# Filler blocks in quarters between the steps of the gated heads of a two-block transformer, on one Trainium2 core

## The chip, the cores and the metric

The program runs on one core of a Trainium2 chip. The metric is the device time of the whole program in microseconds, lower is better. The kernel before takes 3076.76 us (median of 3 runs, 3075.69 to 3077.55). The core's engines run side by side and are joined by semaphores only: TensorE (PE in the profile), VectorE (DVE), ScalarE (ACT), GpSimd (POOL) and the queue that loads weights (SP).

## The reference

A first block (two layers of feed-forward, hybrid mixer, feed-forward) is followed by a second one. The change touches only the token mixer of the second block. There the latent tokens (512) and the context tokens (256) go through one projection `w_in`; a latent attention (MLA) and a gated linear attention (GLA) follow, and both are merged under gates:

```
k_nope_c, v_c = mla_keys_values(kv_cc, kv_norm_g, w_ukv)      # context, norm of 2 x 128 features
k_nope, v = mla_keys_values(kv_c, kv_norm_g, w_ukv)           # latent, the same norm
q_nope, q_rope = mla_queries(q_c, q_norm_g, w_uq)             # norm of 3 x 128 features
s_f = gla_final_state(kg_c, vg_c, gf_c, s0)                   # context: states alone
s_b = gla_final_state(flip(kg_c), flip(vg_c), flip(gb_c), s0)
o_gla, _, _ = gla_bidirectional(qg, kg, vg, gf, gb, s_f, s_b) # latent: states and outputs
out_lat = merge_branches(o_mla @ w_br_mla, gla_branch(o_gla, gr, gla_norm_g, w_br_gla), gate_logits, w_out)
```

One direction of a gated head works in chunks of 64 tokens:

```
b_cum = cumsum(g)                                   # g = log_sigmoid(low-rank product + bias) / 16
u = (kc * exp(b_last - b_cum)).T @ vc               # one update per chunk
s = exp(b_last) * s + u                             # chain over the chunks
a = (qc * exp(b_cum)) @ (kc * exp(-b_cum)).T * mask # scores inside a chunk
o = a @ vc + (qc * exp(b_cum)) @ s_in
y = rms_norm(o) * silu(r)                           # per head, over its 128 values
```

There are four heads and two directions, for the context (states only) and for the latent tokens.

## The kernel before, in words

**Blocks.** All large products are cut into blocks of 1024 rows x 256 columns of weights (1 MB each, `raw`, four slots). ACT writes the high part of a block (`split_hi`, L919), POOL the low part (`split_lo`, L403), and TensorE takes three products for each of 8 x 2 tiles: 48 products of 128x512 (`products`, L452 to L475, lines L468 to L470). Blocks alternate between two places for weights and two pairs of PSUM banks. A half of the weights of block k+2 may be written once block k has passed its middle (`front_done`), the other once it is done (`block_done`). ACT's `evac` of block k writes the first half of block k+2, waits for the end of block k, copies its two results and writes the second half. All these wait in ACT's own order; POOL has one order of splits and of `rms` steps (`rstd`, L408), written out by hand.

**Fillers.** Blocks 8 to 13 and 21 to 29 are independent of the heads and are set between their steps. `FILLERS[u]` lists those of head u (0 to 3 context, 4 to 7 latent tokens), `KVX_FILLER` and `QX_FILLER` are those inside which the column sums of the two norms lie. Fillers 9 to 13 and 27 to 29 are gate logits, copied and spilled by a DMA from ACT; 21 to 26 are the keys, queries, values and `gr` of the next heads.

**Context head u** on TensorE (`gla_context`): a filler; a wait for the state chain of the head before; `gla_updates`, that is three groups of transposes (`turn`, L692), a wait for ACT's copies of them (`turn_ready`) and the update products (L717); `gla_pre` of the next head (decay product, L698); a second filler, if there is one. After head 1 come block 11 with the column sums of the keys' norm, its rows, and a wait for the normed keys (`kvn_ready`); after head 2 block 13 with the queries' norm and a wait for `qn_ready`. The norm itself is DVE's `norm_split`.

**Token head h** on TensorE (`gla_tokens`, u = 4 + h): a filler, in whose middle the rows of the norm of the head before are made (`rms_rows`, L506); turns, wait, updates; the second filler; a wait for the first direction's chain, the score products (L741); a wait for both chains and for the masked scores (`am_ready`); the outputs (L748, L752); the decay product of the next head; the column sums of this head's norm (`rms_cols`, L487), which wait for ACT's square of the outputs. ACT per head: `gla_decays` (three exponentials), filler, `gla_turned` (copies of the turns), filler, square and copy of the outputs, `gla_logs` of the next head (abs, exp, ln). DVE per head: `gla_chain` (two chains of 8 steps, L1680 and L1687), masks (L1720, L1723), `rms_var`, `gla_cumulate` of the next head (L1641 to L1653), `gla_out` (L1708, L1711), `gla_weigh` (L1662 to L1668). After head 3 follow block 29 with the rows of its norm, and the branch products (L899).

## Time and profile before

| | |
|---|---|
| median of 3 runs | 3076.76 us |
| profiled execution | 3074.51 us, span 3072.7 us |
| TensorE busy | 2875.3 us (94%), mean granted clock 0.957 |
| DVE, ACT, POOL busy | 1463.0 (48%), 997.7 (32%), 1132.7 us (37%) |
| context heads | about 2026 to 2148 us |
| token heads | about 2394 to 2585 us |

A busy share is a mean over the whole program. Idle time of TensorE inside the two stretches is read from its waits and from its timeline. The granted clock is the share of full speed (2.4 GHz) at which TensorE ran in a stretch.

### The profile page before, as it was taken

The numbers are of one execution on the slowest core, as the hardware profiler recorded it, in microseconds if no ns is written. First come the engines' busy times: TensorE is split into PE (matmuls) and PEld (weight loads), VectorE is DVE, ScalarE is ACT, GpSimd is POOL, SyncE is SP. The second block draws the span as 40 slices with busy tenths as digits, with TensorE's granted clock in tenths as the row PEclk, the third lists the DMA queues.
The fourth block names the chain that finished last, engine by engine and source line by source line (L and its number), as shares of the span: only waits on it lengthen the run. The fifth ranks groups of instructions, "written<-read, shape, count | busy, mean of one in ns | idle before, by whom it ended". The sixth has DMA issues, their size and how long they took to land.

```text
span 3072.7 us, 36418 instructions
## 1 busy us (share of the span) xinstructions
PE 2875.3 (94%) x12748; PEld 2290.3 (75%) x12748; DVE 1463.0 (48%) x2627; ACT 997.7 (32%) x1409; POOL 1132.7 (37%) x488
## 2 busy tenths in 40 slices
PE   7999999899999999999899999897788899999998
PEld 4888877688887888877678888775444777788886
DVE  3534366452525525265644335625454445563735
ACT  2222235332223322235432222342333443242422
POOL 2444443244444444443244444442111213334443
PEclk9999999999999999999999999897899888999998
DMA  6535442243535435352135344432000113322221
GB/s 247 205 112 184 143 151 69 83 137 137 183 141 197 139 135 190 138 179 81 43 116 188 133 163 165 162 126 77 28 28 28 55 41 130 123 83 94 97 96 41
DMA packets 69266, 374.32 MB, mean 122 GB/s; under 512 B 7776, under 2 KB 8544, under 8 KB 38656
## 3 DMA queue, kind: packets, MB, share of 16 engines
q1 hardware_dynamic: 65424, 359.61, 33.3%
q10 hardware_dynamic: 3696, 12.85, 1.1%
q8 instruction: 81, 1.33, 0.2%
q14 instruction: 65, 0.53, 0.1%
HBM read 364.04 MB, written 8.39 MB: 121 GB/s over the span
## 4 chain that ended last, share of the span: by engine, by line
PE 39%; issue 32%; POOL 19%; DVE 4%; ACT 2%; DVEq 1%; ACTq 1%; SPq 1%; DMA 1%; POOLq 0%
POOL w_lo L403 19%; PE psum L468 10%; PE psum L469 10%; PE psum L470 10%; PE psum L850 1%; PE psum L828 1%; PE psum L717 1%; PE psum L752 1%; PE psum L840 1%; DVE psum L1842 1%; PE psum L698 1%; ACT w_hi L919 0%; PE psum L901 0%; PE psum L899 0%; PE psum L900 0%
## 5 line engine op out<-in xcount | busy, mean ns | idle before, releaser
L403 POOL TENSOR_TENSOR w_lo<-raw,w_hi 128x1024 fp32r<-128x1024 f32 x464 | 1114.1, 2407 | 1769.5 <-ACT w_hi L919 1769.5
L468 PE MATMUL psum<-h_hi,w_hi 128*128 128x512 f32 x2256 | 898.4, 398 | 25.5 <-DVE h_lo L1363 16.6
L469 PE MATMUL psum<-h_lo,w_hi 128*128 128x512 f32 x2256 | 891.5, 395 | 0.0
L470 PE MATMUL psum<-h_hi,w_lo 128*128 128x512 f32 x2256 | 889.8, 394 | 0.0
L919 ACT CAST w_hi<-raw 128x1024 fp32r<-128x1024 f32 x464 | 482.2, 1048 | 941.7 <-PE psum L470 815.3
L468 PEld LDWEIGHTS psum<-h_hi,w_hi 128*128 128x128 f32 x2256 | 432.3, 192 | 122.9 <-DVE h_lo L1363 15.8
L470 PEld LDWEIGHTS psum<-h_hi,w_lo 128*128 128x128 f32 x2256 | 431.6, 191 | 91.4
L469 PEld LDWEIGHTS psum<-h_lo,w_hi 128*128 128x128 f32 x2256 | 432.6, 192 | 89.9 <-issue 0.5
L468 PE MATMUL psum<-hid_hi,w_hi 128*128 128x512 f32 x880 | 350.4, 398 | 4.7 <-DVE hid_lo L1848 4.7
L470 PE MATMUL psum<-hid_hi,w_lo 128*128 128x512 f32 x880 | 350.1, 398 | 0.0
L469 PE MATMUL psum<-hid_lo,w_hi 128*128 128x512 f32 x880 | 350.1, 398 | 0.0
L1390 DVE SCALAR_TENSOR_TENSOR x<-psum,gate,x 128x512 f32<-128x512 f32 x128 | 90.2, 747 | 390.7 <-PE psum L470 355.4
L1304 DVE SCALAR_TENSOR_TENSOR psum<-mod_raw,psum 128x512 f32<-128x512 f32 x336 | 255.5, 760 | 37.8 <-issue 18.5
L1408 DVE TENSOR_TENSOR psum<-act_ring,psum 128x512 f32<-128x512 f32 x88 | 61.3, 696 | 403.6 <-ACT act_ring L941 403.6
L468 PEld LDWEIGHTS psum<-hid_hi,w_hi 128*128 128x128 f32 x880 | 166.7, 189 | 46.1 <-DVE hid_lo L1848 6.0
L469 PEld LDWEIGHTS psum<-hid_lo,w_hi 128*128 128x128 f32 x880 | 166.7, 189 | 40.1
L470 PEld LDWEIGHTS psum<-hid_hi,w_lo 128*128 128x128 f32 x880 | 166.5, 189 | 40.2
L941 ACT ACTIVATE act_ring<-psum 128x512 f32<-128x512 f32 x88 | 52.7, 599 | 372.2 <-PE psum L470 372.1
L1842 DVE SCALAR_TENSOR_TENSOR psum<-gpad,cpar,psum 128x441 f32<-128x441 f32 (+2 forms) x176 | 123.2, 700 | 13.6 <-issue 0.6
L408 POOL TENSOR_TENSOR rstd<-var,mhalf 128x4 f32<-128x4 f32 x18 | 18.5, 1029 | 158.0 <-DVE var L1341 158.0
L1415 DVE TENSOR_TENSOR hid_lo<-psum,hid_hi 128x512 fp32r<-128x512 f32 x88 | 60.5, 688 | 31.9 <-ACT hid_hi L947 31.9
L1321 DVE CUSTOM_DVE_ANT_0 mod_acc<-psum,ident 128x128 f32<-128x128 f32 x208 | 54.1, 316 | 34.4 <-DMA alibi<-in_alibi_dram 14.8
(337 smaller groups left out, 2843.4 us busy)
## 6 DMA issues: line engine op xcount, KB each, us to landing
raw<-in_weights_dram SPq DMA_DIRECT2D x232, 1024.0 KB, 5.6
mod_raw<-in_mod_w_dram SPq DMA_DIRECT2D x192, 512.0 KB, 4.2
first_mods_a<-in_mod_w_dram SPq DMA_DIRECT2D x8, 512.0 KB, 11.8
first_mods_b<-in_mod_w_dram SPq DMA_DIRECT2D x8, 512.0 KB, 15.3
first_mods_a<-gate_spill ACTq DMA_DIRECT2D x4, 1024.0 KB, 10.8
gate_spill<-gate_out_c ACTq DMA_DIRECT2D x5, 512.0 KB, 3.0
x<-in_xT_dram SPq DMA_DIRECT2D x1, 2048.0 KB, 8.7
x_spill<-x ACTq DMA_DIRECT2D x1, 2048.0 KB, 11.5
```

Source lines behind the costliest of these rows:

```text
L403: pool.tensor_tensor(w_lo[:, k % 2, cs], raw[:, k % 4, cs], w_hi[:, k % 2, cs].bitcast(F32), ALU.subtract).then_inc(lo_ready, 1)
L468: pe.matmul(out, wh, rhs_hi[:, c, :], start=(c == ks[0]), stop=False)
L469: pe.matmul(out, wh, rhs_lo[:, c, :], start=False, stop=False)
L470: mm = pe.matmul(out, wl, rhs_hi[:, c, :], start=False, stop=(c == ks[-1]))
L919: act.copy(w_hi[:, k % 2, cs], raw[:, k % 4, cs]).then_inc(hi_ready, 1)
L941: act.activation(act_ring[:, j % 2, :], psum[:, 2 * (k % 2), :], ACT.Silu).then_inc(silu_ready, 1)
L1304: o = dve.scalar_tensor_tensor(macc, w, cond_ps[:, k:k + 1], macc, ALU.mult, ALU.add)
L1321: dve.tensor_tensor_reduce(mod_acc[:, t * P:(t + 1) * P], psum[:, bank, t * P:(t + 1) * P], ident[:, :], 1.0, 0.0, ALU.mult, ALU.add, mod_ ...
L1390: o = dve.scalar_tensor_tensor(x[:, m, :], psum[:, 2 * (k % 2) + t, :], gate[:, m:m + 1], x[:, m, :], ALU.mult, ALU.add)
L1408: dve.tensor_tensor(ps, act_ring[:, j % 2, :], ps, ALU.mult).then_inc(prod_ready, 1)
L1415: dve.tensor_tensor(hid_lo[:, j, :], ps, hid_hi[:, j, :].bitcast(F32), ALU.subtract).then_inc(hid_ready, 1)
L1842: dve.scalar_tensor_tensor(dst[:, rs, cs], src[:, rr, cc], tap(3 * (dy + 1) + dx + 1), dst[:, rs, cs], ALU.mult, ALU.add)
```

## The change

The fillers are dealt out anew. A new helper `quarters` issues a block in parts of 12 products, so that small steps can stand between parts. In the token heads the first filler is run by `beside_norm`, which sets the column sums of the head before behind its first quarter and the rows behind its third; `gla_updates` is cut in two, `gla_turns` and `gla_updates`, with the first quarter of the second filler between; the second quarter stands ahead of the scores, the last two behind them. The decay product of the next head now stands ahead of the outputs; on ACT `gla_logs` stands ahead of the square. On DVE the variance step lies inside `gla_cumulate`. In the context heads every head has one filler, blocks 10 and 12 carry the norms' column sums, and the waits for `kvn_ready` and `qn_ready` stand behind the next filler. POOL's order of `rms` steps and splits follows the blocks.

```diff
-FILLERS = ((8, 9), (10,), (12,), (), (21, 22), (23, 24), (25, 26), (27, 28, 29))
-KVX_FILLER, QX_FILLER = 11, 13
+FILLERS = ((8,), (9,), (11,), (13,), (21, 22), (23, 24), (25, 26), (27, 28, 29))
+KVX_FILLER, QX_FILLER = 10, 12
 ...
-            for r, k, n in (..., (R_KVC, 8, 5), (R_KVX, 13, 2), (R_QX, 15, 8)):
+            for r, k, n in (..., (R_KVC, 8, 4), (R_KVX, 12, 2), (R_QX, 14, 9)):
 ...
+            def quarters(g, k, qs, rhs):
+                for q in qs:
+                    wait_block(g, k, q // 2)
+                    if q == 0:
+                        pe.wait_ge(out_free[k % 2], 2 * g + k // 2 + 1)
+                    for c in (2 * q, 2 * q + 1):
+                        for t in range(2):
+                            wh, wl = (w[:, k % 2, c * 256 + t * P:c * 256 + (t + 1) * P] for w in (w_hi, w_lo))
+                            out = psum[:, 2 * (k % 2) + t, :]
+                            pe.matmul(out, wh, rhs[0][:, c, :], start=(c == 0), stop=False)
+                            pe.matmul(out, wh, rhs[1][:, c, :], start=False, stop=False)
+                            mm = pe.matmul(out, wl, rhs[0][:, c, :], start=False, stop=(c == KC - 1))
+                    if q == 1:
+                        mm.then_inc(front_done, 1)
+                    if q == 3:
+                        mm.then_inc(block_done, 1)
 ...
             def gla_context(u):
-                if len(FILLERS[u]) > 0:
-                    products(G2, FILLERS[u][0], hx)
+                products(G2, FILLERS[u][0], hx)
                 if u:
                     pe.wait_ge(chain_ready, 2 * u)
-                gla_updates(u, gv_c[:, u, :], TC)
+                if u == 2:
+                    pe.wait_ge(kvn_ready, 2)
+                if u == 3:
+                    pe.wait_ge(qn_ready, 1)
+                gla_turns(u, gv_c[:, u, :], TC)
+                gla_updates(u, TC)
                 if u < 3:
                     gla_pre(u + 1, glow_c, TC)
-                if len(FILLERS[u]) > 1:
-                    products(G2, FILLERS[u][1], hx)
+
+            def beside_norm(k, h):
+                quarters(G2, k, (0,), hx)
+                if h >= 0:
+                    rms_cols(R_GLA + h, T, ssq, O_BANK)
+                quarters(G2, k, (1, 2), hx)
+                if h >= 0:
+                    rms_rows(R_GLA + h, T, O_BANK - 1)
+                quarters(G2, k, (3,), hx)
 
             def gla_tokens(h):
                 u, pairs = 4 + h, T // P
-                products(G2, FILLERS[u][0], hx, between=(lambda: rms_rows(R_GLA + h - 1, T, O_BANK - 1)) if h else None)
-                gla_updates(u, gv[:, h % 2, :], T)
-                products(G2, FILLERS[u][1], hx)
+                beside_norm(FILLERS[u][0], h - 1)
+                gla_turns(u, gv[:, h % 2, :], T)
+                quarters(G2, FILLERS[u][1], (0,), hx)
+                gla_updates(u, T)
+                quarters(G2, FILLERS[u][1], (1,), hx)
                 pe.wait_ge(chain_ready, 2 * u + 1)
 ...
                 mm.then_inc(a_ps, 1)
+                quarters(G2, FILLERS[u][1], (2, 3), hx)
                 pe.wait_ge(chain_ready, 2 * u + 2)
                 pe.wait_ge(am_ready, h + 1)
+                if h < GLA_HEADS - 1:
+                    gla_pre(u + 1, krope, T)
 ...
                 mm.then_inc(og_ps, 1)
-                if h < GLA_HEADS - 1:
-                    gla_pre(u + 1, krope, T)
-                rms_cols(R_GLA + h, T, ssq, O_BANK)
 ...
-            products(G2, FILLERS[7][2], hx, between=lambda: rms_rows(R_GLA + GLA_HEADS - 1, T, O_BANK - 1))
+            beside_norm(FILLERS[7][2], GLA_HEADS - 1)
 ...
                 filler(FILLERS[u][1])
+                if h < GLA_HEADS - 1:
+                    gla_logs(u + 1, T)
                 act.wait_ge(og_ps, h + 1)
                 act.activation(ssq[:, :], psum[:, T_BANK, :], ACT.Square)
 ...
-                if h < GLA_HEADS - 1:
-                    gla_logs(u + 1, T)
 ...
                 dve.tensor_tensor(prod[:, :, W], t_ring[:, :, W], act_ring[:, :, W], ALU.subtract)
                 dve.drain()
+                if meanwhile is not None:
+                    meanwhile()
 ...
-                    gla_cumulate(u + 1, T)
+                    gla_cumulate(u + 1, T, lambda: rms_var(R_GLA + h, T, P, O_BANK))
```

## Rows read from the trace of the kernel before

**Rows 1.** The page: busy us (share of the span) x instructions.
```profile
PE 2875.3 (94%) x12748; PEld 2290.3 (75%) x12748; DVE 1463.0 (48%) x2627; ACT 997.7 (32%) x1409; POOL 1132.7 (37%) x488
```
**Rows 2.** TensorE's waits, 2340 to 2620: us in total, times, longest.
```profile
PE psum L717 <- ACTq L1114: 10.7, 4, 3.2
PE psum L748 <- DVE am L1723: 10.4, 4, 3.6
...
PE psum L692 <- DVEq L1663: 2.9, 1, 2.9
```
**Rows 3.** TensorE's waits, 2000 to 2160.
```profile
PE psum L717 <- ACTq L1114: 8.8, 4, 2.6
PE psum L692 <- DVEq L1663: 7.6, 1, 7.6
PE psum L468 <- DVEq L1599: 5.8, 1, 5.8
```
**Rows 4.** Windows: us; busy of PE, PEld, DVE, ACT, POOL; clock; DMA share, GB/s.
```profile
503.00:519.00 16.00, 15.94 (x86) 11.95 (x88) 12.52 (x29) 7.41 (x25) 4.80 (x2) 1.00 0.19 67
2412.00:2459.00 47.00, 39.64 (x218) 33.15 (x217) 23.28 (x35) 20.48 (x24) 10.94 (x5) 0.89 0.13 45
2505.00:2555.00 50.00, 45.00 (x215) 37.08 (x214) 23.28 (x35) 20.49 (x24) 10.93 (x5) 0.80 0.15 53
```
**Rows 5.** TensorE's timeline, token heads: start us, duration, instruction, [idle before].
```profile
2387.39 0.39 PE L468 MATMUL psum<-h_hi,w_hi 128*128 128x512 f32 x1
...
2392.83 0.39 PE L468 MATMUL psum<-h_hi,w_hi 128*128 128x512 f32 x1
...
2393.52 0.60 PE L692 MATMUL psum<-ident,gv 128*128 128x128 f32 x4
...
2397.53 3.27 PE L717 MATMUL psum<-gvt,kdT 64*128 64x128 f32 x32 [2.54 <-ACTq L1114]
...
2412.14 1.95 PE L741 MATMUL psum<-qe,kn 128*128 128x128 f32 x16
2416.32 1.13 PE L748 MATMUL psum<-am,gvt 128*128 128x128 f32 x8 [2.24 <-DVE am L1723]
...
2422.81 1.05 PE L487 MATMUL psum<-ones,ssq 128*128 128x1 f32 x8
...
2555.48 1.95 PE L741 MATMUL psum<-qe,kn 128*128 128x128 f32 x16
...
2585.31 0.40 PE L899 MATMUL psum<-om_hi,w_hi 128*128 128x512 f32 x1
```
**Rows 6.** ACT's timeline between token heads 0 and 1.
```profile
2415.06 1.04 ACT L919 CAST w_hi<-raw 128x1024 fp32r<-128x1024 f32 x1 [0.23 <-issue]
...
2422.92 1.27 ACT L1092 ACTIVATE act_ring<-psum,par 128x512 f32<-128x512 f32 x2 [0.63 <-PE psum L698]
...
2429.03 1.28 ACT L1101 ACT_TABLE_LOAD   x1
```
**Rows 7.** Timelines of DVE and, last, POOL, token heads 0 and 1.
```profile
2399.46 1.62 DVE L1687 SCALAR_TENSOR_TENSOR states<-states,prod,psum 128x128 f32<-128x128 f32 x4
...
2429.04 1.41 DVE L1641 TENSOR_SCALAR t_ring<-psum,par 128x512 f32<-128x512 f32 x2 [4.98 <-ACT act_ring L1096]
...
2435.72 0.75 DVE L1708 SCALAR_TENSOR_TENSOR y_gla<-o_sb,par,psum 128x512 f32<-128x512 f32 x1 [0.19 <-issue]
...
2439.98 2.85 DVE L1667 SCALAR_TENSOR_TENSOR qe<-gq,prod 128x512 f32<-128x512 f32 x1
...
2439.84 5.20 POOL L403 TENSOR_TENSOR w_lo<-raw,w_hi 128x1024 fp32r<-128x1024 f32 x2 [14.69 <-ACT w_hi L919]
```
**Rows 8.** Timelines of DVE (first) and TensorE, context heads 1 and 2.
```profile
2053.60 0.76 DVE L1653 TENSOR_TENSOR t_ring<-act_ring 128x256 f32<-128x256 f32 x2
...
2097.72 0.80 PE L468 MATMUL psum<-h_hi,w_hi 128*128 128x512 f32 x1 [5.78 <-DVEq L1599]
...
2110.35 0.38 PE L692 MATMUL psum<-ident,gv_c 128*128 128x128 f32 x2
```

More of the change, by code:

```diff
@@ L427, in _ @@
                         splits(g, k0 + 1, blocks)
-            for r, k, n in ((R_FINAL1, 1, 0), (R_CTX, 1, 4), (R_X1, 5, 3), (R_KVC, 8, 5), (R_KVX, 13, 2), (R_QX, 15, 8)):
+            for r, k, n in ((R_FINAL1, 1, 0), (R_CTX, 1, 4), (R_X1, 5, 3), (R_KVC, 8, 4), (R_KVX, 12, 2), (R_QX, 14, 9)):
                 rms(r)
@@ L700, in gla_pre, with gla_turns @@
                 mm.then_inc(pre_ps, 1)
-            def gla_updates(u, v_src, width):
+            def gla_turns(u, v_src, width):
                 pairs = width // P
-                kt, vt = (kdT, gvt) if width == T else (kdT_c, vt_c)
                 pe.wait_ge(qk_ready, u + 1)
@@ L712, in gla_updates @@
                 turn(psum[:, T_BANK + 1, :], t_ring[:, 1, :], pairs).then_inc(turn_ps, 1)
+            def gla_updates(u, width):
+                pairs = width // P
+                kt, vt = (kdT, gvt) if width == T else (kdT_c, vt_c)
                 pe.wait_ge(turn_ready, u + 1)
@@ L782, in _ @@
                     rms_rows(R_KVX, T)
-                    pe.wait_ge(kvn_ready, 2)
                 if u == 2:
@@ L786, in _ @@
                     rms_rows(R_QX, T)
-                    pe.wait_ge(qn_ready, 1)
             pe.wait_ge(chain_ready, 8)
@@ L1117, in gla_context @@
                 gla_decays(u, TC)
-                if len(FILLERS[u]) > 0:
-                    filler(FILLERS[u][0])
+                filler(FILLERS[u][0])
                 gla_turned(u, TC)
@@ L1122, in gla_context @@
                     gla_logs(u + 1, TC)
-                if len(FILLERS[u]) > 1:
-                    filler(FILLERS[u][1])
             def gla_tokens(h):
@@ L1631, in final_and_ctx_norm, with gla_cumulate @@
                 whole_norm(48, range(3, DC))
-            def gla_cumulate(u, width):
+            def gla_cumulate(u, width, meanwhile=None):
                 h, chunks = u % 4, width // GLA_CHUNK
@@ L1731, in gla_tokens @@
                     dve.drain()
-                rms_var(R_GLA + h, T, P, O_BANK)
                 if last:
+                    rms_var(R_GLA + h, T, P, O_BANK)
                     for c in range(GLA_HEADS - 1):
```

## The prediction

> **What bounds the kernel now.** Read the busy shares first: TensorE is busy 94% of the span [rows 1]. So only what leaves TensorE idle, or running at the lower of its two clock levels, can be won; a faster DVE, ACT or POOL is worth nothing unless TensorE waits for it. Then the waits of TensorE, cut to the two stages that the diff touches. In the gated heads of the latent tokens TensorE stood 10.7 us for the copies of the turned operands (`turn_ready`), 10.4 us for the masked scores (`am_ready`) and 2.9 us for the weighted keys (`qk_ready`) [rows 2]. In the four context heads it stood 7.6 us in one piece ahead of head 3's turns, 5.8 us in one piece ahead of the filler product of head 2, and 8.8 us in four waits for turned copies [rows 3]. Then the granted clock: 0.89 over one head's 47 us and 0.80 over another's 50 us, against 1.00 in a stretch of the mixer where quarters of a block alternate with small matmuls [rows 4]. With two levels, 2.4 and 1.2 GHz, 0.89 means 22% of the time at the lower one, 0.80 means 40%. Last the timelines of each engine over one head, for the sums below [rows 5 to 7].
>
> **The pieces on TensorE at the full level** [rows 5]. 24 products take 2392.83 - 2387.39 = 5.44 us, so a quarter (12) takes 2.7; I book 2.8, since each quarter begins behind small matmuls, and 5.5 for two together. Turns 1.5 us; updates 3.2 (x32, 3.27 with the overlap at their end); scores 1.95; outputs and decay product (`gla_pre`) together 2422.81 - 2416.32 = 6.5, of which 1.9 the decay product; column sums (`rms_cols`) 0.9 and rows (`rms_rows`) 0.8, each 1.05 with its overlap.
>
> **First token head, from its turns to the end of its second filler.** Turns 1.5. A quarter now stands between turns and updates; before, TensorE stood from the end of the turns to 2397.53, 4.0 us after the turns began at 2393.52. Turns and quarter are 4.3 us, so that wait is gone. Updates 3.2. Next a quarter of 2.8, then the wait for the first direction's state chain, which DVE starts halfway through the updates. Eight steps of 0.4 (states row of [rows 7]: 1.62 us for four, plus a copy of 0.3) are 3.4 us; from halfway that is 1.8 us behind the updates, inside the quarter's 2.8. Scores 1.95, two quarters 5.5. DVE's second chain (3.4) and its mask operations (2.2, the gap from the scores' end at 2412.14 + 1.95 to the outputs at 2416.32) end about 2.5 us before the quarters do, so the `am_ready` stall is gone as well. Sum 1.5 + 2.8 + 3.2 + 2.8 + 2.0 + 5.5 = 17.8.
>
> **One period, from the end of a second filler to the end of the next** (t = 0 at the start). The decay product stands first, 1.9, then outputs to 6.5, a quarter to 9.3. Now the column sums need ACT's square, and ACT is in order: the evacuation of the filler, from TensorE's end at 2412.14 to the end of the cast at 2415.06 + 1.04, occupies it to t = 4.0; the decay logs moved ahead of the square take 2422.92 to 2429.03, 6.1 us, to t = 10.1; then the square, 0.6 [rows 6]. Column sums at 10.9: a **new wait of 1.6 us**. Sums to 11.8, two quarters to 17.3, rows to 18.1, a quarter to 20.9. DVE: logs ready at 10.1, cumulation 6.6 us (2429.04 to about 2435.6, with the variance now inside it, 0.2), the norm and the weighing of keys 3.0 us (2435.72 to TensorE's turns at 2438.73) after the rows at 18.2: turns can start at 21.2, a **new wait of 0.3** [rows 7]. Turns to 22.7, quarter to 25.5 (ACT's turned copies are ready near 25.0: its decays end at 19.8, then a cast, two copies, a cast and three copies follow), updates 28.7, quarter 31.5, scores 33.5, quarters 39.0. DVE's query and key products run into POOL's splits there and end near 27.5; its chains then end at 31.0 and 34.4, the masks at 36.5: no wait. Three periods are 117.0, where the trace has 143.3 from 2412.14 to its third successor.
>
> **Last head**: outputs 4.6, quarter 2.8, sums 0.9, two quarters 5.5, rows 0.8, quarter 2.8, and 0.4 for the last norm and split (3.3 us on DVE behind the rows, a quarter of 2.8 and the sum's latency over it): 17.8. **Stage**: 17.8 + 117.0 + 17.8 = 152.6 against 2585.31 - 2393.52 = 191.8 [rows 5]: 39.2 us less, if the clock stays at the full level. It won't wholly. A drop came once a stall had preceded small matmuls; two of the three kinds of stall go, but pre, outputs and the 1.6 us wait lie close together, and at the lower level outputs and pre take 6.5 us longer together at worst. Bounds: nothing (the mixer's 1.00), or all of what was lost before, some 19 us (0.11 and 0.20 of 47 and 50 us [rows 4], less where TensorE was idle anyway, over four heads). I take 6, nearer the mixer row, whose pattern this becomes: **33 us**.
>
> **Context heads.** The fillers move so that a whole one stands behind each norm: block 11 between the norm of the keys and head 2's turns, block 13 between the norm of the queries and head 3's. A filler is 10.9 us; the waits are 5.8 and 7.6 [rows 3]: both covered, -13.4. Head 3 had no filler ahead of its turns, and its wait for the turned copies was 8.8 - 3 x 2.6 = 1.0; with a filler to evacuate first it becomes the 2.6 of the others: +1.6. Behind the 5.8 us stall 48 products took 2110.35 - 2097.72 = 12.6 us instead of 10.9 [rows 8]: -1.7. Head 1 loses one of two fillers: its keys must be weighed within the 10.9 us of block 9. Before, its cumulation was done at 2053.60 + 0.76 = 2054.4 [rows 8], and exponential and weighing (0.63 + 0.76) would have been done by 56.0, but ACT took them only behind the second filler; now ACT takes them at once, 2 us before TensorE arrives at about 58.1: no wait. The POOL passes and weight loads move along with their blocks; each split has the same lead of a block as before. The two waits moved from behind the norms to ahead of the turns queue only the turns behind them. Sum **-13.5 us**; bounds -10 (block 9 just misses) and -17 (the slow turns and updates behind the 7.6 us stall recover too).
>
> **Forecast.** 33.2 + 13.5 = 46.7. The profiled execution took 3074.5 us (span 3072.7); the median of the runs is 3076.8, 2.3 above it. 3074.5 - 46.7 = 3027.8, as a run 3030.
>
> **A rule weighed.** Between abs, exp and ln ACT shows 6.1 us for 1.27 + 1.28 + 1.06 + 1.28 + 1.06 = 5.95: the two table loads cost 1.3 us each and nothing more [rows 6]. The Trainium skill (ScalarE: Activation LUTs, What ACT_TABLE_LOAD costs) adds a drain of about 1.38 us to every switch. By it the square, now behind both, would come 2.8 us later in each of three heads, 8.3 us, and the time would be 3038; the trace decides against it. Should the square itself need a load behind ln (behind silu it didn't), that is 1.3 us a head.
>
> **Rivals.** (1) *The weighing falls behind POOL's split.* With POOL at work (5.2 us for two) one DVE product of two SBUF operands takes 2.85 us instead of 0.69 [rows 7]. In my sum the weighing ends 0.1 us after the cast that releases POOL, its last operation having begun 0.5 us before it. If the rows come 0.6 us later, the weighing loses one or two such operations, 2.2 to 4.9 us, in three heads: 6.6 to 15 us, 3037 to 3045. For it: the margin is thin, a short spell at the lower clock uses it up. Against: ACT's cast then starts no earlier, and before the change the order held in each of three heads. The Trainium skill (SBUF — State Buffer, Who interferes with whom) has this as an exclusive lock, taken by whoever issues first, for two-input operations too; by that rule, with which the 2.85 us agree, the loser waits whole operations, and the time is this rival's. (2) *The square is the new bound.* If the clock falls at every decay product, the outputs end later, but the square is bound by ACT; the pieces behind it run slow, some 6 us a head instead of 2: 18 more, the time 3042 to 3048. For it: 0.80 in the third head. Against: the stall that opened those spells is gone. (3) *Slower.* Cut into quarters, the products no longer hold the clock: each of the 432 products of nine blocks would cost another 0.227 us, 98 us in all. The gain before any clock loss, 39.2 + 13.5 = 52.7, is used up from 232 products at the lower level; with all of them the time is 3076.8 - 53 + 98 = 3122. For it: 0.80. Against: the mixer's quarters at 1.00. (4) *The filler hides nothing*, since DVE, not order, is the bound and the stalls move to the column sums: 3065 to 3080. Against: DVE is busy 23.3 us of 47 [rows 4].
>
> **How the numbers follow.** Forecast 0.62, with its own range 3022 to 3038; rival 1 0.14, rival 2 0.15, rival 3 0.04, rival 4 0.05. Range 3020 to 3046: it leaves out the two last, part of rival 2, and a gain beyond full clock and the context's upper bound. Within 0.2% is 3070.6 to 3082.9, about what a measurement can tell from no change: part of rival 4, 0.03. Slower 0.04 (rival 3), faster 0.93.
>
> **What would show it.** In the trace after: the waits for `am_ready` and of the updates in the token heads gone; a wait of column sums for ACT's square, 1 to 2.5 us, in heads 1 to 3; block ends 39 to 42 us apart; no wait of over 4 us in the context heads; four waits of 2.6 us for turned copies there. It is wrong if the turns wait more than 2 us, if the clock in the heads stays under 0.9, or if head 1's context turns wait for their weighed keys.

## The result

The changed kernel takes 3019.47 us (median of 4 runs, 3019.32 to 3021.84) against 3076.69 us before (median of 4 runs with the one made beside it). The ratio is 0.9815, 95% interval 0.9804 to 0.9827: 57.2 us less. I had forecast 3030 with a range of 3020 to 3046. The direction was right; the time lies 0.5 us below the range and 10.5 us below the forecast.

Where the time went is read from four marks in both traces: the first context decay product, the first value product behind the context heads, the first turn of token head 0, and the first branch product.

| stretch | before | after | difference | forecast |
|---|---|---|---|---|
| context heads | 2025.90 to 2147.82 = 121.9 | 2025.75 to 2130.68 = 104.9 | 17.0 | 13.5 |
| attention (unchanged code) | 2147.82 to 2393.52 = 245.7 | 2130.68 to 2376.15 = 245.5 | 0.2 | 0 |
| token heads | 2393.52 to 2585.31 = 191.8 | 2376.15 to 2532.20 = 156.1 | 35.7 | 33.2 |
| behind them (unchanged code) | 2585.31 to 3072.7 = 487.4 | 2532.20 to 3017.7 = 485.5 | 1.9 | 0 |

With 0.2 us ahead of the context heads that is the 55.0 us between the spans. The other 2.2 us between the medians are no change of the kernel: the profiled execution of before (3074.5) lay 2.2 us under its own median, that of after (3019.5) lay on it.

TensorE's waits in the token heads of the changed kernel, over 2330 to 2535 us (line, releaser: us in total, times, longest), answer to [rows 2]:

```profile
PE psum L710 <- DVEq L1696: 2.9, 3, 2.3
PE psum L505 <- ACTq L1167: 2.8, 3, 1.0
PE psum L487 <- ACTq L1091: 2.7, 1, 2.7
PE psum L777 <- DVEq L1729: 2.1, 2, 1.2
PE psum L933 <- DVEq L1771: 0.4, 1, 0.4
PE psum L716 <- DVE am L1756: 0.2, 1, 0.2
```

The update products (L739 now) no longer wait for turned copies. The masked scores (am) cost 0.2 us instead of 10.4. New are the waits of the column sums (L505) for ACT's square, 0.8 to 1.0 us in each of three heads, which the prediction had, and two waits of the scores (L777) for the state chain, which it had not. The turns (L710) wait 0.3 us in two heads as booked, and 2.3 us in head 3, where 0.3 was booked. In the context heads, over 2000 to 2160 us, answering to [rows 3]:

```profile
PE psum L739 <- ACTq L1148: 10.3, 4, 2.6
...
PE psum L831 <- DVEq L1729: 3.5, 1, 3.5
```

The waits for the two norms are gone, and head 3's wait for copies is as long as the others' now. The granted clock, as in [rows 4] (us; busy of PE, PEld, DVE, ACT, POOL; clock; DMA share, GB/s): before over the whole stretch of the token heads, then after over the same.

```profile
2394.00:2585.00 191.00, 166.34 (x857) 140.38 (x855) 90.30 (x143) 70.16 (x85) 43.66 (x20) 0.85 0.14 50
```
```profile
2376.00:2532.00 156.00, 147.78 (x862) 121.16 (x860) 88.52 (x143) 70.42 (x86) 46.47 (x20) 0.97 0.17 61
```

0.85 of 191 us means 57 us at the lower level, 0.97 of 156 means 9. The three periods, from decay product to decay product (in the last to the outputs of head 3, which has none), took 40.8, 38.3 and 42.7 us. The second on TensorE (start, duration, instruction, idle before):

```profile
2433.34 1.95 PE L716 MATMUL psum<-mod_acc,gates_all 32*128 32x512 f32 x4 [0.21 <-DVE am L1756]
...
2443.47 1.05 PE L505 MATMUL psum<-ones,ssq 128*128 128x1 f32 x8 [0.77 <-ACTq L1167]
...
2454.06 0.66 PE L710 MATMUL psum<-ident,gv 128*128 128x128 f32 x4 [0.30 <-DVEq L1696]
...
2458.30 2.06 PE L739 MATMUL psum<-gvt,kdT 64*128 64x128 f32 x32
2460.28 0.50 PE L487 MATMUL psum<-h_hi,w_hi 128*128 128x512 f32 x1
...
2464.18 2.05 PE L777 MATMUL psum<-qe,kn 128*128 128x128 f32 x16 [0.89 <-DVEq L1729]
...
2471.64 1.98 PE L716 MATMUL psum<-mod_acc,gates_all 32*128 32x512 f32 x4
```

This period took 38.3 us, where I had booked 39.0. The column sums come 10.1 us behind the decay product (10.9 booked), the turns 20.7 (21.2). The other two are longer: the three together took 121.8 us, where 117.0 were booked and, for the whole stage, 6 for the clock. In the first and in the third the two quarters behind the column sums ran in part at the lower level. Windows from the column sums to the rows, in the first period and then in the second:

```profile
2402.93:2411.02 8.09, 8.09 (x33) 6.66 (x34) 5.81 (x8) 3.86 (x5) 1.85 (x1) 0.79 0.02 7
2443.47:2449.96 6.49, 6.49 (x33) 5.51 (x34) 5.82 (x8) 2.25 (x3) 1.85 (x1) 1.00 0.02 6
```

In the third period they took 8.09 us again, and behind the turns' wait of 2.3 us the way from turns to updates took 5.85 us instead of 4.24. That is three times 1.6 us at the lower level, 4.8 in all. The updates take 2.0 us, not the 3.2 that I had read from [rows 5].

### The profile page after: what moved, and what is told of

It is laid out like the page before. It is cut to its first block, busy times and chain, and to the rows that moved or that the text cites. A ratio compares the mean times of both kernels' runs of the same rounds, so it can differ in the third digit from the quotient of the medians.

```text
span 3017.7 us, 36418 instructions
## 1 busy us (share of the span) xinstructions
PE 2846.8 (94%) x12748; PEld 2261.4 (75%) x12748; DVE 1463.1 (48%) x2627; ACT 997.9 (33%) x1409; POOL 1136.1 (38%) x488
## 4 chain that ended last, share of the span: by engine, by line
PE 39%; issue 33%; POOL 20%; DVE 4%; ACT 2%; DVEq 1%; ACTq 1%; DMA 1%; SPq 1%; POOLq 0%
POOL w_lo L403 20%; PE psum L468 10%; PE psum L470 10%; PE psum L469 10%; PE psum L884 1%; PE psum L862 1%; PE psum L487 1%; PE psum L488 1%; PE psum L489 1%; PE psum L874 1%; DVE psum L1875 1%; PE psum L933 1%; PE psum L935 0%; PE psum L934 0%; SPq L364 0%
## 5 line engine op out<-in xcount | busy, mean ns | idle before, releaser
L468 PE MATMUL psum<-h_hi,w_hi 128*128 128x512 f32 x2112 | 833.3, 395 | 17.2 <-DVE h_lo L1394 16.6
L469 PE MATMUL psum<-h_lo,w_hi 128*128 128x512 f32 x2112 | 829.1, 393 | 0.0
L470 PE MATMUL psum<-h_hi,w_lo 128*128 128x512 f32 x2112 | 828.3, 392 | 0.0
L468 PEld LDWEIGHTS psum<-h_hi,w_hi 128*128 128x128 f32 x2112 | 401.5, 190 | 106.9 <-DVE h_lo L1394 15.9
L469 PEld LDWEIGHTS psum<-h_lo,w_hi 128*128 128x128 f32 x2112 | 401.5, 190 | 83.8 <-issue 0.5
L470 PEld LDWEIGHTS psum<-h_hi,w_lo 128*128 128x128 f32 x2112 | 400.9, 190 | 84.6
## 6 DMA issues: line engine op xcount, KB each, us to landing
first_mods_a<-gate_spill ACTq DMA_DIRECT2D x4, 1024.0 KB, 10.9
```

The source lines that it names most:

```text
L468: pe.matmul(out, wh, rhs_hi[:, c, :], start=(c == ks[0]), stop=False)
L469: pe.matmul(out, wh, rhs_lo[:, c, :], start=False, stop=False)
L470: mm = pe.matmul(out, wl, rhs_hi[:, c, :], start=False, stop=(c == ks[-1]))
```

## The experiments

Gains below are against the changed kernel's median (3019.5), or, where said, against before's runs on the same chip. Where an edit touches one stage, its stretch in the trace tells more than the total: in these traces the code ahead of the context heads, the attention and the last stage move by 3 to 5 us, though nothing in them was changed.

### Each part alone

`ctx_only` has the change's context heads, waits and POOL order, `tok_only` its token heads; the other stage is as before.

```diff
 # ctx_only: against the kernel before, only this part of the change
-FILLERS = ((8, 9), (10,), (12,), (), ...)
-KVX_FILLER, QX_FILLER = 11, 13
+FILLERS = ((8,), (9,), (11,), (13,), ...)
+KVX_FILLER, QX_FILLER = 10, 12
+                if u == 2:
+                    pe.wait_ge(kvn_ready, 2)
+                if u == 3:
+                    pe.wait_ge(qn_ready, 1)
 # tok_only: all of the change but this part
```

> The context part alone: its fillers, waits and POOL order as in the changed kernel, the token heads as before. Theory A (the two parts are independent, and each is worth what its stretch of the two traces shows): the context stretch was 121.9 us and is 104.9, so 17.0 us less than before, near 3059.7. Theory B (my prediction's term, 13.5 us, with nothing regained behind the 7.6 us stall): near 3063. Rival C (the stretches share something, so that one part alone is worth less): above 3065. In the trace TensorE should have no wait for the normed keys or queries, and four of 2.6 us for turned copies.

> The token part alone: the context heads as before. Theory A: the token stretch was 191.8 us and is 155.5, so 36.3 less, near 3040.4. Theory B (my prediction's term): 33 less, near 3043.5. Rival C: under 30 us less, above 3046. With ctx_only the two gains should add up to the 55 to 57 us of the whole change; if they add up to less than 52, the parts help each other.

Measured: ctx_only 3059.48 us, ratio 0.9945 (0.9928 to 0.9961), 16.1 us under its own runs of before (3075.56). tok_only 3037.91 us, ratio 0.9877 (0.9861 to 0.9894), 37.7 us under them. Theory A holds for both; the sum, 53.8 us, is within the intervals of the whole's 57.2 (each reaches some 5 us to either side). The stretches show the independence more sharply: ctx_only has context heads of 105.2 us and token heads of 191.9 (104.9 after, 191.8 before), tok_only 121.8 and 156.1 (121.9 before, 156.1 after). Both terms of my sum were too small, neither wrong in kind.

### The price of the two norm stalls

```diff
             def gla_context(u):
+                if u == 2:
+                    pe.wait_ge(kvn_ready, 2)
+                if u == 3:
+                    pe.wait_ge(qn_ready, 1)
                 products(G2, FILLERS[u][0], hx)
                 if u:
                     pe.wait_ge(chain_ready, 2 * u)
-                if u == 2:
-                    pe.wait_ge(kvn_ready, 2)
-                if u == 3:
-                    pe.wait_ge(qn_ready, 1)
```

> The changed kernel with its two waits for the normed keys and queries put ahead of their fillers (blocks 11 and 13) again. It prices the two stalls alone, the order of the blocks unchanged. Theory A (a stall costs its own length and a spell at the lower clock behind it): waits of about 5.8 and 7.6 us come back, and the 48 products behind each take 12 to 13 us instead of 10.8; in all 16 to 17 us more than the changed kernel, near 3036. Theory B (the stall's own length is the whole cost): 13.4 us more, near 3032.9. If the waits come out much shorter than 5.8 and 7.6, the order of the blocks had changed their length.

Measured: 3038.81 us, ratio 0.9882 (0.9865 to 0.9898), 19 us more than the changed kernel (two runs near 3036.4 and two near 3041.2; the trace is of one near 3036.4). TensorE's waits over 2000 to 2160 us in this kernel:

```profile
PE psum L468 <- DVEq L1630: 12.4, 2, 6.6
```

and the filler behind the first of them, up to head 2's turns, on its timeline:

```profile
2086.83 0.80 PE L468 MATMUL psum<-h_hi,w_hi 128*128 128x512 f32 x1 [5.78 <-DVEq L1630]
...
2099.69 0.38 PE L710 MATMUL psum<-ident,gv_c 128*128 128x128 f32 x2
```

The stalls are 12.4 us long; the stretch (2025.86 to 2148.86 = 123.0 us) is 18.1 us longer than in the changed kernel. The other 5.7 us stand behind the stalls: 48 products take 12.86 us here and 11.0 without a stall ahead (2080.70 to 2091.71 in the changed kernel's timeline), the second time 12.78. From the rows ahead of a stall to the turns behind its filler the way is 7.9 us longer for the stall of 5.8, and 8.6 for that of 6.6: 1.3 to 1.4 times its length. The last 1.6 us lie between the two, in the decay product and the filler behind head 2's updates; that the stalls caused them is not shown. Theory A, and its price was if anything low.

### A stall ahead of the outputs

```diff
                 gla_updates(u, T)
-                quarters(G2, FILLERS[u][1], (1,), hx)
+                quarters(G2, FILLERS[u][1], (1, 2, 3), hx)
                 pe.wait_ge(chain_ready, 2 * u + 1)
 ...
                 mm.then_inc(a_ps, 1)
-                quarters(G2, FILLERS[u][1], (2, 3), hx)
```

> The changed kernel with all of the second filler's remaining quarters ahead of the scores, so that nothing stands between scores and outputs: the old place of the scores. Theory A (a stall ahead of small matmuls is what lowers the clock, so a stall costs more than its length): waits of 2.2 us for the masked scores come back in four heads, 8.8 us, the scores' waits for the first chain (2.1 us) go; on top the columns and products behind run at the lower clock in most heads, 4 to 8 us: near 3032. Theory B (the clock follows the share of idle time over the whole head, which changes little): the waits' length alone, 6.7 us, near 3026. Rival (the small matmuls themselves lower the clock, stall or not): the clock in the token heads stays at about 0.96 and the time is that of theory B.

Measured: 3040.07 us, ratio 0.9883 (0.9866 to 0.9899), 20.6 us more. Its waits over 2325 to 2545 us, and its clock over the token heads:

```profile
PE psum L716 <- DVE am L1755: 6.7, 3, 2.2
...
PE psum L786 <- DVE am L1755: 3.6, 1, 3.6
PE psum L710 <- DVEq L1695: 3.1, 3, 2.5
```
```profile
2383.00:2549.00 166.00, 152.56 (x792) 128.36 (x791) 86.32 (x137) 67.19 (x79) 43.48 (x19) 0.87 0.16 57
```

The waits came back at 10.3 us. The scores' and column sums' 4.9 us went, and the turns' and the branch products' stayed, so that all waits in the stage grew by 5.4 us (13.8 against 8.4). Yet the stage grew from 156.1 to 176.0 us, by 19.9. The rest is the clock, 0.87 in place of 0.97 over the stage. The outputs show it, first without and then with the drop, in heads 0 and 1 of this one kernel:

```profile
2397.64 3.68 PE L790 MATMUL psum<-qe,states 128*128 128x64 f32 x32
...
2436.64 6.93 PE L790 MATMUL psum<-qe,states 128*128 128x64 f32 x32
```

The work is the same. Behind a stall of 2.24 us the clock held in head 0 and fell in heads 1 and 2; behind the 3.65 us of head 3 it fell too. Theory A had this right and its size too small (8 us at most; some 14). One thing this run does not separate: with the quarters gone, scores and outputs also stand next to each other, so the stall and the longer row of small matmuls came together. Neither decides by itself: in head 0 the same stall ahead of the same row kept the clock.

### The quarter between turns and updates

```diff
-                quarters(G2, FILLERS[u][1], (0,), hx)
                 gla_updates(u, T)
-                quarters(G2, FILLERS[u][1], (1,), hx)
+                quarters(G2, FILLERS[u][1], (0, 1), hx)
```

> The changed kernel without the quarter between turns and updates in the token heads (it stands behind the updates, with the other). Theory A (the quarter hides ACT's copies and nothing else): a wait of 2.5 to 2.8 us for turned copies comes back in four heads, the scores' waits for the first chain (1.2, 0.9) go since two quarters stand there now: 10.5 - 2 = 8 to 9 us more, and up to 4 for the lower clock behind the waits: near 3029. Rival (the waits only move between places and the head stays as long): within 3 us of 3019.5.

Measured: 3027.58 us, ratio 0.984 (0.9823 to 0.9856), 8.1 us more. Of these the token heads have 5.6 (161.7 against 156.1 us); the unchanged attention ahead of them took 249.2 us in this trace instead of 245.5. Waits over 2335 to 2535 us:

```profile
PE psum L739 <- ACTq L1147: 8.6, 4, 2.5
PE psum L505 <- ACTq L1166: 3.1, 3, 1.0
...
PE psum L710 <- DVEq L1695: 0.9, 3, 0.3
```

The waits for copies returned at 8.6 us and the scores' waits went. The rival is out: this is what the quarter hides. And the updates behind such a wait take 3.40 to 3.68 us again, in place of 2.06, a lower-clock time. The stage grew by less than these two (theory A had 8 to 9 us and up to 4 for the clock), since other costs of the changed kernel are missing here: its scores' waits, its two lower-clock spells of 1.6 us behind the column sums, and the 2.0 us of head 3's turns with the spell behind them.

### The order of decay product, logs and square

```diff
 # PE: the decay product behind the outputs; ACT: gla_logs behind square and copy
-                if h < GLA_HEADS - 1:
-                    gla_pre(u + 1, krope, T)
                 out = psum[:, T_BANK, :]
 ...
                 mm.then_inc(og_ps, 1)
+                if h < GLA_HEADS - 1:
+                    gla_pre(u + 1, krope, T)
 # DVE: rms_var ahead of gla_cumulate
```

> The changed kernel with the next head's decay product behind the outputs again, the logs behind the square on ACT, and the variance ahead of the cumulation on DVE. Theory A (the end of the chain logs, cumulation, norm, weighing sets when the turns start): the column sums no longer wait (1.0 us less), but the logs end about 2.5 us later, and the turns wait about 3 us instead of 0.3: 1 to 2 us more a head, 3 to 5 in all, near 3023.5. Rival (the square bounds the head): 1 us less in each of three heads, near 3016.5.

Measured: 3023.45 us, ratio 0.9818 (0.9801 to 0.9834), 4.0 us more. By medians that is theory A's figure, but the intervals overlap, and the stage doesn't bear it out. Waits moved as theory A has it: the column sums wait for nothing, the turns 5.1 us in three heads (2.9 at most) instead of 2.9, the updates 0.9 us. Yet the token heads took 156.1 us (2380.84 to 2536.95), as in the changed kernel. The first branch product starts 4.7 us later only because the stage begins 4.7 us later, behind stretches that this edit does not touch (2.4 us ahead of the context heads, 2.3 in them). So the order of decay product, logs and square is worth nothing that these runs can show; neither theory holds.

### POOL's split and head 3's weighing

ACT must wait for `yg_ready` before it casts behind blocks 23 and 25, and not before 27, a gate block. The prediction had overlooked that wait; it made the order of weighing and split safe in heads 1 and 2 and not in head 3.

```diff
                 if k in GATE_K:
 ...
+                    if k == 27:
+                        act.wait_ge(yg_ready, 3)
```

> The changed kernel; ACT waits for the gated output of head 2 (yg_ready) before it casts the weights behind block 27, as it already must before blocks 23 and 25. Nothing else differs between head 3 and heads 1 and 2, whose turns wait 0.3 us where head 3's wait 2.3. Lock theory: the cast, and with it POOL's split, starts 1.3 us later, behind the weighing; the weighing takes 1.3 us again instead of 3.3, the turns wait 0.3 us, and the time falls by about 2 us, more by what TensorE loses at the lower clock behind that wait: near 3016.5. Rival (head 3's weighing is slow for another reason, or the wait is of ACT's making): no change, 3019.5.

Measured: 3020.86 us, ratio 0.9813 (0.9797 to 0.983): no change of the time that the runs can tell. In the changed kernel the weighing of head 3 (DVE, L1695) beside POOL's split:

```profile
2492.87 3.26 DVE L1695 TENSOR_TENSOR t_ring<-t_ring,gk 128x512 f32<-128x512 f32 x2
```
```profile
2492.41 2.57 POOL L403 TENSOR_TENSOR w_lo<-raw,w_hi 128x1024 fp32r<-128x1024 f32 x1 [6.00 <-ACT w_hi L953]
```

and with the hold, DVE, then POOL:

```profile
2494.69 1.29 DVE L1697 TENSOR_TENSOR t_ring<-t_ring,gk 128x512 f32<-128x512 f32 x2
2496.11 2.71 DVE L1702 SCALAR_TENSOR_TENSOR qe<-gq,prod 128x512 f32<-128x512 f32 x1
```
```profile
2495.89 5.17 POOL L403 TENSOR_TENSOR w_lo<-raw,w_hi 128x1024 fp32r<-128x1024 f32 x2 [6.06 <-ACT w_hi L953]
```

and two of its waits of TensorE over 2335 to 2535 us:

```profile
PE psum L777 <- DVEq L1731: 3.5, 3, 1.3
...
PE psum L710 <- DVEq L1698: 0.9, 3, 0.3
```

The lock theory is right on its mechanism: moved behind the weighing, the split leaves it 1.29 us, and the turns wait 0.3 us. The split now meets the first query and key products, 2.71 and 2.87 us (0.69 and 2.85 in the changed kernel), and the chain behind them is late, so 2.0 us less ahead of the turns became 1.4 us more ahead of the scores. The turns no longer run at the lower level either, and from head 3's rows to the first branch product the way is 1.9 us shorter (40.2 us against 42.1), which is what the theory had. The whole stage took 152.6 us against 156.1; the other 1.6 us are the lower-clock spell ahead of head 3's rows, which is missing here and which the edit does not touch. The total hides both: the context heads began 2.9 us later and the last stage took 2.7 us longer (488.2 us against 485.5), in unchanged code. The Trainium skill (SBUF — State Buffer, Who interferes with whom) says that whoever issues first holds the shared ports for the whole instruction; the rows shown here agree.

### Copies ahead of the filler's evacuation, and a version that beats both

`turned_first` lets ACT copy the turned operands before it evacuates the filler, so that its casts, and POOL's splits, come later, and puts a quarter between turns and updates in the context too.

```diff
 # ACT, context and token heads
-                filler(FILLERS[u][0])
                 gla_turned(u, width)
+                filler(FILLERS[u][0])
 # PE, context heads
-                products(G2, FILLERS[u][0], hx)
+                quarters(G2, FILLERS[u][0], (0, 1, 2), hx)
 ...
                 gla_turns(u, gv_c[:, u, :], TC)
+                quarters(G2, FILLERS[u][0], (3,), hx)
                 gla_updates(u, TC)
```

> The changed kernel, but on ACT the copies of the turned operands stand ahead of the evacuation of the filler in all eight heads, and in the context heads the filler's last quarter stands between turns and updates. Lock theory (POOL's split, released by ACT's cast, blocks two-input DVE operations; released later it meets nothing that TensorE waits for): the waits of the turns (0.3, 0.3, 2.3 us) shrink to 0.3 each and the waits of the scores for the first chain (1.2, 0.9) go, some 4 us. Cover theory for the context: the four waits of 2.6 us go, 10 us, less a possible 1.3 us in head 1, whose keys have less time. Together 12 to 14 us less than the changed kernel, near 3006. Rival (the evacuation, now later, holds up the weight splits of the block after next): TensorE waits for low parts, and the time stays at 3015 or above.

Measured: 3008.81 us, ratio 0.978 (0.9763 to 0.9796), 10.7 less than the changed kernel (9.2 between the spans). The context stretch gave 15.0 us (2026.77 to 2116.74 = 90.0 against 104.9) and the token heads 1.6 (2366.46 to 2520.90 = 154.4 against 156.1); the start 1.0 us later and the last stage 2.1 us longer took 3.1. The attention between, unchanged code, took back 4.2 us (2116.74 to 2366.46 = 249.7 against 245.5). In the context heads no turned copies are waited for any more, and head 1's turns wait 0.8 us for their keys. A window over the same part of it, the changed kernel and then this one:

```profile
2131.00:2337.00 206.00, 166.76 (x573) 85.99 (x573) 97.23 (x166) 67.10 (x124) 23.78 (x10) 0.92 0.08 27
```
```profile
2117.00:2327.00 210.00, 170.73 (x572) 88.97 (x572) 97.32 (x166) 67.01 (x123) 23.77 (x10) 0.91 0.09 31
```

TensorE is busy for 3.97 us longer with the same work and stands no longer; the matmuls themselves were slower, at a clock of 0.91 instead of 0.92. Why the lower clock came there and not in the changed kernel stays open; no_turn_cover, with the changed kernel's context heads, has 249.2 us in this stretch, so it comes without this edit too. In the token heads the turns wait 0.3 us each, as expected; the scores' waits did not go but moved: 3.8 us in four heads. The copy that starts the first state chain is an SBUF to SBUF operation and now met the split (0.23 us in head 1 of the changed kernel):

```profile
2411.85 1.44 DVE L1714 COPY states<-mod_raw 128x128 f32<-128x128 f32 x1 [2.90 <-PE psum L739]
```

So `best1` copies both starting states before DVE waits for the updates, and puts the column sums behind two quarters.

```diff
             def gla_chain(u, width):
+                if full:
+                    for d in range(2):
+                        dve.tensor_copy(states[:, d, d * (chunks - 1), :], s0[:, 4 * d + h, :])
+                    dve.drain()
                 for d in range(2):
                     dve.wait_ge(u_ps[d if full else 1], u + 1)
-                    if full:
-                        dve.tensor_copy(states[:, d, order[0], :], last)
-                        dve.drain()
 ...
             def beside_norm(k, h):
-                quarters(G2, k, (0,), hx)
+                quarters(G2, k, (0, 1), hx)
                 if h >= 0:
                     rms_cols(R_GLA + h, T, ssq, O_BANK)
-                quarters(G2, k, (1, 2), hx)
+                quarters(G2, k, (2,), hx)
```

> turned_first with two more edits: DVE copies the starting states of both directions before it waits for the updates, and the column sums stand behind two quarters instead of one. In turned_first the scores waited 0.8 to 1.1 us in all four heads (the copy of the starting state took 1.44 us, blocked by POOL's split), the column sums 1.0 us in three. Lock theory: the copy done early meets no split, the chain starts with the updates, the scores' waits (3.8 us) go. Order theory: with the column sums later their wait (3.1 us) goes, the rows come a little earlier. Together 5 to 8 us less than turned_first (3008.8): near 3002. Rival (the chain from the logs to the weighing, which neither edit shortens, holds the turns): the 3 us of the column sums come back as waits of the turns, 3005.

Measured: 2997.27 us, ratio 0.9739 (0.9723 to 0.9755), 11.5 less than turned_first, more than expected. The token heads have 9.7 of it (144.7 us against 154.4): 4.8 us of waits (3.4 left of 8.2), the rest the clock. What each of the two edits gave alone was not measured. Waits over 2335 to 2535 us, and the clock over its token heads, 145 us in place of 156:

```profile
PE psum L487 <- ACTq L1092: 2.7, 1, 2.7
PE psum L934 <- DVEq L1773: 2.0, 1, 2.0
PE psum L710 <- DVEq L1697: 1.4, 3, 0.5
```
```profile
2363.00:2508.00 145.00, 141.79 (x863) 118.17 (x861) 75.10 (x141) 72.77 (x89) 47.07 (x21) 1.00 0.19 66
```

The clock is whole, 1.00. `best2` adds two edits:

```diff
-            pe.wait_ge(g_in, 1)
-            pe.wait_ge(o_mla_ready, 4)
             for h in range(GLA_HEADS):
                 gla_tokens(h)
 ...
+                if h == 0:
+                    pe.wait_ge(g_in, 1)
+                    pe.wait_ge(o_mla_ready, 4)
                 gla_turns(u, gv[:, h % 2, :], T)
 # beside_norm: the column sums of the last head behind one quarter, of the others behind two
```

> best1 with two more edits: the waits for the first head's values (g_in, 2.7 us of TensorE) and for o_mla stand ahead of the turns of token head 0, behind block 21, not ahead of it; and the column sums of the last head stand behind one quarter again (in best1 the branch products waited 2.0 us). If both waits are hidden: 2.7 + 1.6 us less and 1 to 2 us for the slow products behind the first, near 2991.5. Rival (ACT evacuates block 20 and casts only then, so the turns of head 0 wait in its place): about 2995.

Measured: 2993.82 us (2989.35 to 2995.29), ratio 0.9729 (0.9713 to 0.9745). Both waits are gone from its trace but for 0.4 us, and attention and token heads together are 4.8 us shorter than in best1 (387.4 against 392.2). Against best1 the intervals overlap; against the changed kernel it is 25.7 us less.

## Why the prediction was right and where it failed

**Which waits go.** Right in the main: in the token heads the waits for turned copies and for the masked scores went, in the context heads those for both norms; head 3 of the context got its 2.6 us, and head 1 of the context did not wait for its keys. The decay product ahead of the outputs brought the wait of the column sums (1.0 us of the 1.6 booked). One sign that was to show the forecast wrong did come: head 3's turns waited 2.3 us, over the 2 named.

**The steps that failed** are two terms of the sum, and both leave out what runs at the lower clock behind a wait. In the token heads it is "Updates 3.2", in the list of pieces at the full level. 3.27 us is the duration of [rows 5], and it stood right behind a 2.54 us stall: a lower-clock duration taken for a full-clock one. The windows over these 32 updates, before and then after, have granted clocks of 0.59 and 1.00:

```profile
2397.53:2400.80 3.27, 3.27 (x33) 3.05 (x33) 1.34 (x5) 0.00 (x0) 0.88 (x1) 0.59 0.38 103
```
```profile
2458.30:2460.30 2.00, 2.00 (x34) 1.88 (x33) 2.00 (x3) 0.00 (x0) 0.72 (x1) 1.00 0.28 49
```

The token stage was booked at 152.6 + 6 = 158.6 us and took 156.1, 2.5 less. The updates are 4.8 of it in four heads; the clock cost 4.7 us (0.97 of 156) where 6 were booked, 1.3 less; the waits were 8.4 us where 6.1 were (three of 1.6, three of 0.3 and 0.4), 2.3 more; and 1.3 more lies in small differences that I did not follow one by one. In the waits the column sums' 2.0 us less and head 3's turns' 2.0 us more cancel, and the 2.1 us of the scores are left. They come from the same term: in the second period DVE's first chain ended 30.7 us behind the decay product, as booked (31.0), but TensorE was there at 29.9 instead of 31.5.

**The second, and the largest by itself,** is the recovery in the context: -13.5 booked, 17.0 measured. The two stalls, with what stands behind the first, came out as booked (7.7 and 7.7 us for 7.5 and 7.6), and so did head 3's longer wait. 1.6 us more are head 3's turns and updates, which stood behind the 7.6 us stall at the lower level; I had named them only as a bound. Another 1.6 us lie in the decay product and the filler behind head 2's updates (2114.81 to 2131.03 = 16.2 us before, 2096.17 to 2110.80 = 14.6 after), behind the same wait of 2.55 us in both kernels; these I had not named at all. So the total met the bound of -17, but only half for the reason given with it. Such a spell is not fixed by the code: logs_back has the changed kernel's context heads and took 107.2 us in them instead of 104.9, with 2.08 us for the update products of heads 2 and 3 where the changed kernel has 1.16.

**The rest** of the 10.5 us, 4.5, is no step of the change: 2.2 us by which the profiled execution of before lay under its median, added to a forecast that needed no such step, and 2.3 us in code that did not change. The last stage, from the branch products to the end, took 484.2 to 488.2 us in twelve traces, of kernels that all share its code, and the unchanged attention 244.4 to 249.7 us in eleven; a forecast from one profile can't be better than that. With 0.5 us between the time and the range, such chance alone could have put it inside.

**The rivals.** Rival 1 (weighing behind the split) happened in one head of three, 2.0 us, and not for the reason I gave: in head 3 nothing holds ACT's cast back behind the gated output of head 2. Rival 2 is out as priced; that a stall opens a spell at the lower clock is what the old order lost by, as scores_late shows. Rival 3 is the reverse of what came: with quarters among the small matmuls and shorter stalls the clock is 0.97, with whole blocks and stalls between it was 0.85. Rival 4 is out. The rule on table loads (the Trainium skill, ScalarE: Activation LUTs, What ACT_TABLE_LOAD costs), which adds a drain of about 1.38 us to each, is contradicted here. The first and the last of six rows of ACT in the changed kernel, abs and the square of token head 0:

```profile
2396.30 1.26 ACT L1126 ACTIVATE act_ring<-psum,par 128x512 f32<-128x512 f32 x2
...
2402.28 0.58 ACT L1166 ACTIVATE ssq<-psum 128x512 f32<-128x512 f32 x1
```

The square starts 5.98 us after abs, and abs, the two loads and the two functions between are 1.26 + 1.28 + 1.06 + 1.28 + 1.06 = 5.94 us. The square behind ln needed no load of its own.

## What to carry to other kernels

Before adding up pieces, read the granted clock over each row that is used: one that stands right behind a stall can be a lower-clock duration (updates 3.27 us at 0.59, 2.06 at 1.00), and a change that removes the stall then shortens it too. Price a stall of TensorE of 5.8 to 6.6 us ahead of a whole block at 1.3 to 1.4 times its length. For one of 2 to 3 us no single price holds: behind the same wait of 2.56 us the update products of head 3 took 1.16 us in the changed kernel and 2.08 in logs_back, and in scores_late the clock took more than the stalls themselves. Spread independent products in parts between the small steps, each part as long as the wait that it covers. Judge an edit to one stage by that stage's stretch in the trace and not by the total alone: the total of hold27 hid a stage shorter by 3.5 us, and that of logs_back showed 4.0 us that its stage does not have. When a blocked operation is moved out of the way of another engine, look at what it meets next: here 2.0 us less ahead of the turns brought 1.4 us more ahead of the scores.

## What the hardware showed that I had not expected

A stall of 2.24 us ahead of 6.5 us of small matmuls was followed by the lower clock in two heads of three in scores_late and not in the first, with the same work and the same stall. Two rows of one kernel, 3.68 and 6.93 us for the same 32 matmuls, are this. Even a wait of 1.02 us can stand ahead of such a spell: behind it the same two quarters took 8.09 us in two heads of the changed kernel, and 6.50 us in all three heads of no_turn_cover. With no stall over 0.5 us between the steps the clock stayed at 1.00 through 145 us, though the small steps fill more than a third of them.
